# The last block of four down projections run as two column halves, with the norm chain and the next stage's entry beside the second half

## What is computed

```python
# first block, twice (i = 0: convolution, i = 1: differential attention)
f = swiglu(rms_norm(h, g0), w_gu, w_down);  h = h + 0.5 * rms_norm(f, g1)
m = mixer(rms_norm(h, g2));                 h = h + rms_norm(m, g3)
f = swiglu(rms_norm(h, g4), w_gu, w_down);  h = h + 0.5 * rms_norm(f, g5)
# second block, once
h = h + mix(rmsnorm(h, g6) @ w_in) @ w_out  # gated linear attention and dilated attention
h = h + square(relu(rmsnorm(h, g7) @ w_ff1)) @ w_ff2;  out = rmsnorm(h, g8)
```

## Time and profile before

| | |
|---|---|
| median of 3 runs (lowest, highest) | 1375.8 us (1375.73, 1375.89) |
| the profiled execution, its span | 1376.72 us, 1375.0 us |
| PE matmul busy | 1356.9 us, 99% of the span, 11028 records |
| PE weight loads busy | 1331.0 us, 97% |
| VectorE, ScalarE, GpSimd busy | 885.3 us (64%), 653.0 us (47%), 13.5 us (1%) |
| the chain that ended last | PE 94%, VectorE 3%, ScalarE 2%, DMA 1% |
| HBM | 225.49 MB read, 165 GB/s over the span |

### The profile page before, as it was taken

How to read it: one execution, slowest core, us unless ns; L and a number is a source line. 1 busy time by engine, 2 the same in 40 slices (tenths; PEclk the granted TensorE clock), 3 DMA queues, 4 the chain that set the end, 5 groups by cost and what they waited for, 6 DMA issues and landing times.

```text
span 1375.0 us, 26722 instructions
## 1 busy us (share of the span) xinstructions
PE 1356.9 (99%) x11028; PEld 1331.0 (97%) x11028; DVE 885.3 (64%) x1306; ACT 653.0 (47%) x927; POOL 13.5 (1%) x27
## 2 busy tenths in 40 slices
PE   8999999999999999999999999999999999999997
PEld 8999999999999999999999999999999999999997
DVE  6666548767666547666547897866645767777543
ACT  5444445436444445344445666644445545644332
POOL 0000000000000000000000000000001000000000
PEclk9999999999999999999999999999999999999999
DMA  7545553334445543445553323455645513455550
GB/s 285 184 166 204 202 192 139 138 123 153 171 167 216 181 147 128 162 175 210 182 190 133 123 93 124 153 184 183 234 180 195 200 62 114 163 184 183 184 184 31
DMA packets 30415, 227.68 MB, mean 166 GB/s; under 512 B 3489, under 2 KB 5089, under 8 KB 6529
## 3 DMA queue, kind: packets, MB, share of 16 engines
q1 hardware_dynamic: 28768, 223.88, 45.5%
q0 software_dynamic: 720, 1.82, 0.4%
q10 hardware_dynamic: 848, 0.87, 0.2%
HBM read 225.49 MB, written 1.06 MB: 165 GB/s over the span
## 4 chain that ended last, share of the span: by engine, by line
PE 94%; DVE 3%; ACT 2%; DMA 1%; issue 1%; ACTq 0%; DVEq 0%
PE ps L1701 26%; PE ps L1703 26%; PE ps L1702 26%; PE ps L1741 1%; PE ps L1736 1%; PE ps L1737 1%; ACT w_hi L526 1%; PE ps L1770 1%; PE ps L1761 1%; PE ps L1717 1%; PE ps L1961 1%; PE ps L1759 1%; PE ps L1937 1%; DMA w_raw<-w_gu 1%; PE ps L2200 1%
## 5 line engine op out<-in xcount | busy, mean ns | idle before, releaser
L1009 DVE TENSOR_TENSOR w_lo<-w_raw,w_hi 128x2048 fp32r<-128x2048 f32 (+2 forms) x172 | 439.0, 2553 | 207.6 <-ACT w_hi L526 207.5
L526 ACT ACTIVATE w_hi<-w_raw 128x2048 fp32r<-128x2048 f32 (+2 forms) x178 | 382.1, 2147 | 385.0 <-PE ps L1703 371.8
L1701 PE MATMUL ps<-x_hi,w_hi 128*128 128x272 f32 (+1 forms) x1952 | 561.5, 288 | 0.1
L1703 PE MATMUL ps<-x_hi,w_lo 128*128 128x272 f32 (+1 forms) x1952 | 558.6, 286 | 0.0
L1702 PE MATMUL ps<-x_lo,w_hi 128*128 128x272 f32 (+1 forms) x1952 | 556.9, 285 | 0.0
L1701 PEld LDWEIGHTS ps<-x_hi,w_hi 128*128 128x128 f32 x1952 | 367.9, 188 | 4.4 <-issue 4.0
L1703 PEld LDWEIGHTS ps<-x_hi,w_lo 128*128 128x128 f32 x1952 | 367.9, 188 | 0.0
L1702 PEld LDWEIGHTS ps<-x_lo,w_hi 128*128 128x128 f32 x1952 | 367.6, 188 | 0.1
L1701 PE MATMUL ps<-hid_hi,w_hi 128*128 128x272 f32 (+1 forms) x960 | 274.3, 286 | 0.2 <-DVE w_lo L1009 0.2
L1703 PE MATMUL ps<-hid_hi,w_lo 128*128 128x272 f32 (+1 forms) x960 | 273.6, 285 | 0.0
L1702 PE MATMUL ps<-hid_lo,w_hi 128*128 128x272 f32 (+1 forms) x960 | 272.8, 284 | 0.0
(11 more groups left out here) (308 smaller groups left out, 1416.0 us busy)
## 6 DMA issues: line engine op xcount, KB each, us to landing
w_raw<-w_gu SPq DMA_DIRECT2D x86, 1024.0 KB, 4.9
w_raw<-w_dn SPq DMA_DIRECT2D x32, 1408.0 KB, 6.0
w_raw<-w_ff SPq DMA_DIRECT2D x32, 1024.0 KB, 4.9
w_raw<-w_conv_in SPq DMA_DIRECT2D x8, 1536.0 KB, 6.6
w_raw<-w_qkv SPq DMA_DIRECT2D x8, 1536.0 KB, 6.6
w_raw<-w_mix_in SPq DMA_DIRECT2D x8, 1536.0 KB, 6.6
w_raw<-w_conv_out SPq DMA_DIRECT2D x4, 1024.0 KB, 4.9
w_raw<-w_attn_out SPq DMA_DIRECT2D x4, 1024.0 KB, 4.9
```

Of the source, the lines that this page charges most:

```text
L526: act.activation(w_hi[j % SPLIT][:, 0:width], w_raw[j][:, 0:width], ACT.Copy).then_inc(hi_ready, 1)
L1009: dve.tensor_tensor(w_lo[j % SPLIT][:, 0:width], w_raw[j][:, 0:width], w_hi[j % SPLIT][:, 0:width].bitcast(F32), ALU.subtract).then_inc(lo ...
L1701: pe.matmul(out_ap, w_hi[slot][:, cols], hi(k), start=first, stop=False)
L1703: mm = pe.matmul(out_ap, w_lo[slot][:, cols], hi(k), start=False, stop=last)
```

## The change

In the four ffn sub-blocks u = 0, 2, 3, 5 (CROSSED) the last of the 8 down blocks runs first over the lower half of the columns (136 of 272, or 128 of 256), then over the upper half, into another PSUM bank. The norm chain of the lower half is issued beside the upper half of the block; `sum_first_half` stands ahead of tile k = 5 of the second half. The next stage's entry (`first_block` for conv_in, qkv and mix_in, `first_pair` for the gu stages) goes over the 8 tiles of the lower half and then over those of the upper half, each with its own matmul; `sum_second_half` stands behind its first tile. `keep_warm` is no longer issued in these four places. ScalarE's order there is `crossing`: half-width x_hi tiles with the split of the next block's weights in three (or two) pieces between them. VectorE goes through the 8 tiles twice in half width, with the second half's Newton steps behind the first pass.

In all gu entries but the first (q = 2, 3, 5) the first two weight blocks are laid out anew on the host, as the first stage has them: block 0 holds the tiles k = 0 to 3 of all four outputs, block 1 the tiles k = 4 to 7. Their 96 matmuls stay 96 where no half is cut (q = 2 and 5); only the 16 with w_lo of block 1 stay in full width behind a cut (q = 3). VectorE's first `take` then waits for both blocks.

```diff
--- before.py
+++ after.py
@@ -340,6 +343,14 @@
 
         STATE_BANK = (6, 7, 5)
 
+        CROSSED = (0, 2, 3, 5)
+
+        GU_ENTRIES = (2, 3, 5)
+
+        LAST_BANK = {0: 4, 2: 0, 3: 4, 5: 4}
+
+        SUMS_AT = 5
+
         AHEAD = 4
 
         FIRST_SQUARES = 4
...
@@ -389,6 +400,20 @@
         def first_col(u):
 
             return 0 if u <= 4 else META
+
+        def spans(u):
+
+            c0 = META if u >= 4 else 0
+            mid = (c0 + T) // 2
+            return [(c0, mid), (mid, T)] if u in CROSSED else [(c0, T)]
+
+        def h_done(q):
+
+            return sum(KD * len(spans(u)) for u in range(q))
+
+        def x_done(q):
+
+            return KD + h_done(q - 1) if q > 0 else 0
 
         def loop(eng, count, body, first=0, peel=0):
 
...
@@ -598,6 +640,48 @@
                 act.activation(fx[:, m if isinstance(m, int) else bass.ds(m, 1), c0:T], ps[:, j, c0:T],
                                ACT.Copy, scale=g).then_inc(f_ready, 1)
 
+            def crossing(u, post, pre):
+
+                (c0, mid), _ = spans(u)
+                at, m, q, bank = CROSSED.index(u) + 1, KD - 1, u + 1, LAST_BANK[u]
+                pre_g, post_g = COL[pre], par[:, COL[post] + m:COL[post] + m + 1]
+                last_square = square[m % 2]
+
+                def x_part(i, k):
+                    a, b = spans(u)[i]
+                    act.wait_ge(h_ready, h_done(u) + KD * i + k + 1)
+                    act.activation(x_hi[:, k, a:b], h[:, k, a:b], ACT.Copy, scale=par[:, pre_g + k:pre_g + k + 1])\
+                       .then_inc(x_hi_ready, 1)
+
+                act.wait_ge(sumsq_ready, KD * u + m)
+                act.wait_ge(last_half, at)
+                act.activation(last_square[:, c0:mid], ps[:, m % 4, c0:mid], ACT.Square).then_inc(half_sq_ready, 1)
+                act.wait_ge(half_summed, at)
+                act.activation(r0[:, c0:mid], ps[:, SUM + 1, c0:mid], ACT.Abs_reciprocal_sqrt, scale=1.0 / D, bias=eps_col)\
+                   .then_inc(half_r0_ready, 1)
+                act.activation(fx[:, m, c0:mid], ps[:, m % 4, c0:mid], ACT.Copy, scale=post_g).then_inc(half_f_ready, 1)
+                x_part(0, 0)
+                x_part(0, 1)
+                act.wait_ge(block_used, FIRST[ENTER[q]])
+                act.activation(last_square[:, mid:T], ps[:, bank, mid:T], ACT.Square).then_inc(f_sq_ready, 1)
+                x_part(0, 2)
+                second_hi_part(q, 0)
+                root(None, mid, SUM, sumsq_summed, u + 1)
+                x_part(0, 3)
+                x_part(0, 4)
+                second_hi_part(q, 1)
+                act.activation(fx[:, m, mid:T], ps[:, bank, mid:T], ACT.Copy, scale=post_g).then_inc(f_ready, 1)
+                x_part(0, 5)
+                x_part(0, 6)
+                if WIDTH[FIRST[ENTER[q]] + 1] == 3 * KD * P:
+                    second_hi_part(q, 2)
+                x_part(0, 7)
+                for k in range(KD + 1):
+                    if k < KD:
+                        x_part(1, k)
+                    if k > 0:
+                        h_square(q, k - 1, c0)
+
...
@@ -1081,27 +1169,70 @@
                     qkv_lo(2, 0, 1)
                 root(s, c0, SUM)
 
...
+                if crossed:
+                    first_root()
+                else:
+                    root(s, spans(u)[0][0], SUM + 1)
+                for i, (a, b) in enumerate(spans(u)):
+                    if i == 1:
+                        dve.wait_ge(rstd_ready, s + 1)
+                    for k in range(KD + 2):
+                        if k < KD:
+                            if crossed and k == KD - 1:
+                                dve.wait_ge(half_f_ready if i == 0 else f_ready, at + 1 if i == 0 else KD * (u + 1) + F_CREDIT)
+                            if k >= 2:
+                                dve.wait_ge(h_ready, base + KD * i + k - 1)
+                            dve.tensor_tensor(scaled[k % 2][:, a:b], fx[:, k, a:b], rstd[:, a:b], ALU.mult)\
+                               .then_inc(scaled_ready, 1)
+                        if crossed and i == 0 and k >= KD - 1:
+                            second_root(k - KD + 1)
                         if k >= 2:
...
+                            lo_part(u + 1, k - 2, a, gain, b, i)
+                        if k < KD:
+                            dve.wait_ge(scaled_ready, base + KD * i + k + 1)
+                            dve.scalar_tensor_tensor(out=h[:, k, a:b], in0=scaled[k % 2][:, a:b], scalar=factor,
+                                                     in1=h[:, k, a:b], op0=ALU.mult, op1=ALU.add).then_inc(h_ready, 1)
 
...
@@ -1723,31 +1854,62 @@
                 pe.wait_ge(h_sq_copied, q + 1)
                 pe.matmul(ps[:, SUM, c0:T], ones[:, :], h_sum[:, c0:T], start=True, stop=q < 8).then_inc(h_sq_summed, 1)
 
-            def first_block(q, n0, parts, ahead=()):
-
+            def first_block(q, n0, parts):
 
                 split_ready(n0, 0)
...
+                ranges = spans(q - 1) if q < 7 else [(META, T)]
+                for i, (a, b) in enumerate(ranges):
+                    for k in range(KD):
+                        pe.wait_ge(x_hi_ready, x_done(q) + KD * i + k + 1)
+                        for s, (o, c) in enumerate(parts):
+                            cols, r = slice((s * KD + k) * P, (s * KD + k + 1) * P), slice(max(a, c), b)
+                            to = o[:, r.start - c:r.stop - c]
+                            pe.matmul(to, w_hi[0][:, cols], x_hi[:, k, r], start=i == 0 and k == 0, stop=False)
+                            pe.matmul(to, w_lo[0][:, cols], x_hi[:, k, r], start=False, stop=False)
+                        if i == 0 and k == 0 and len(ranges) > 1:
+                            sum_second_half(q - 1)
+                        pe.wait_ge(x_lo_ready, x_done(q) + KD * i + k + 1)
+                        for s, (o, c) in enumerate(parts):
+                            cols, r = slice((s * KD + k) * P, (s * KD + k + 1) * P), slice(max(a, c), b)
+                            to = o[:, r.start - c:r.stop - c]
+                            mm = pe.matmul(to, w_hi[0][:, cols], x_lo[:, k, r], start=False, stop=i == len(ranges) - 1 and k == KD - 1)
+                mm.then_inc(block_used, 1)
+
+            def first_pair(q, n0, c0):
+
+                outs = [ps[:, bank, :] for bank in (AHEAD, AHEAD + 1, 2, 3)]
+                tile_at = lambda k, s: slice((k % (KD // 2) * 4 + s) * P, (k % (KD // 2) * 4 + s + 1) * P)
+                split_ready(n0, 0)
+                ranges = spans(q - 1)
+                for i, (a, b) in enumerate(ranges):
+                    for k in range(KD):
+                        slot = k // (KD // 2)
+                        if i == 0 and k == KD // 2:
+                            pe.wait_ge(half_hi_ready, GU_ENTRIES.index(q) + 1)
+                        if i == 0 and k == KD // 2 + 2:
+                            pe.wait_ge(hi_ready, n0 + 2)
+                        pe.wait_ge(x_hi_ready, x_done(q) + KD * i + k + 1)
+                        for s, o in enumerate(outs):
+                            pe.matmul(o[:, a:b], w_hi[slot][:, tile_at(k, s)], x_hi[:, k, a:b], start=i == 0 and k == 0, stop=False)
+                            if slot == 0:
+                                pe.matmul(o[:, a:b], w_lo[0][:, tile_at(k, s)], x_hi[:, k, a:b], start=False, stop=False)
+                        if i == 0 and k == 0 and len(ranges) > 1:
+                            sum_second_half(q - 1)
+                        pe.wait_ge(x_lo_ready, x_done(q) + KD * i + k + 1)
+                        for s, o in enumerate(outs):
+                            mm = pe.matmul(o[:, a:b], w_hi[slot][:, tile_at(k, s)], x_lo[:, k, a:b], start=False, stop=False)
+                        if i == len(ranges) - 1 and k == KD // 2 - 1:
+                            mm.then_inc(block_used, 1)
+                group_squares(q, c0)
+                split_ready(n0, 1)
+                for k in range(KD // 2, KD):
+                    for s, o in enumerate(outs):
+                        mm = pe.matmul(o[:, c0:T], w_lo[1][:, tile_at(k, s)], x_hi[:, k, c0:T], start=False, stop=k == KD - 1)
+                    if k == KD // 2 + 1:
+                        sum_groups(q, c0)
+                mm.then_inc(block_used, 1)
+
+            def second_block(q, n0, outs, c0, late=False):
 
                 pe.wait_ge(hi_ready, n0 + 2)
                 if not late:
...
@@ -1828,13 +1986,40 @@
                     before = (lambda k: pe.wait_ge(hid_lo_ready, KF * f + k + 1) if k >= KF - 4 else None) if j == 0 else None
                     product(ps[:, j, c0:T], j % 2, 0, KF, hi, lo, before=before).then_inc(block_used, 1)
 
-                loop(pe, DN_N, step)
+                loop(pe, DN_N - 1 if u in CROSSED else DN_N, step)
+                if u in CROSSED:
+                    (a, mid), _ = spans(u)
+                    m = DN_N - 1
```

(26 more changed lines are left out.)

151 lines of the change are left out of this document (84 added, 67 removed).

## The result

The changed kernel takes 1412.4 us (four runs, 1412.40 to 1412.59) against 1375.85 us (four runs, 1375.73 to 1376.05): +36.6 us, a ratio of 1.0265 [1.0253, 1.0277]. Forecast were 1413.5 us and a range of 1400 to 1434.

A forecast was written before the change was run, and what follows sets the result against it. PE was taken as the bound: matmul count times spacing, plus waits. Terms 55.6 - 20.25 + 3.6 - 1.3 gave +37.7 us, so 1413.5 us against 1375.8, range 1400 to 1434.

The forecast's parts named there:

- The bound: PE, busy 99% of the span at full clock: time is matmul count times start-to-start spacing, plus PE's waits.
- Halved matmuls, +55.6: Last down blocks and entries: 560 matmuls become 1120, each half costing its 128-column weight load, 0.1115 us: +55.6 us.
- Stretches, -20.25: Four stretches between block and next entry vanish, as PE's upper half covers the lower half's norm chain: -20.25 us.
- Sums, +3.6: The norm's fp32 sum matmuls, now half width and in PE's stream, add 0.9 us at each of four places.
- small waits, -1.3: PE's small waits in the crossed entries go, since half-width VectorE delivers tiles sooner than PE needs them: -1.3 us.
- ScalarE's queue, 0 (up to 4): At the crossings, ScalarE's root waits and split pieces between x_hi tiles delay PE by 0, at most 1 us a place.
- The uncut gu entries, 0 (within 0.5): Entries q = 2 and 5, 96 matmuls before and after, VectorE's first take later: 0, within 0.5 us either way.
- Rival 1: In the halved matmuls fp32r loads hide entirely, halves cost 0.063 us, the chain then bounds: 1372 us, chance 0.07.
- The second: In the halved matmuls partly overlapping loads give a spacing about the break-even, hardly any change: some 1378 us, chance 0.03.
- Rival 3, the clock: PE's clock falls to half speed in the crossings, without empty matmuls and with PE waiting for loads: 1470 us, chance 0.06.

The follow-up runs named there:

- third: Kernel before with only the last down block of the four ffn sub-blocks run in column halves, norm chain still behind both: 1401.5 us, ratio 1.0185.
- fourth experiment: Kernel before with only the entries of conv_in, gu2, qkv and mix_in run in column halves, x tiles still full width: 1407.2 us, ratio 1.0259.
- fifth experiment: Changed kernel with CROSSED empty and the empty matmuls back, so nothing halved, new entry loops and weight layout kept: 1374.7 us, ratio 0.9990.
- first: Kernel before with 80 instead of 26 empty fp32r matmuls in each of six stretches, at 32 to 240 moving columns: 1417.3 us.
- ninth: Changed kernel with the column cut at 96 instead of the middle: 1502.4 us (1484.3 to 1513.9).

## Why the prediction was right, point by point

**The bound.** PE's stream set the time before and sets it after; the earlier trace rows against the page above.

**The segments.** From the first record of one `group_squares` to that of the next, the kernel before against the changed one. The gu entries have 8 more matmuls in front of that mark than before, 1.0 us, which is moved back in the last column but one.

| segment, to stage | before | after | difference, mark moved back | by the prediction's terms |
| --- | --- | --- | --- | --- |
| conv_in (crossed) | 205.23 | 214.24 | +9.01 | +8.97 |
| gu1 | 104.32 | 104.88 | -0.45 | 0 |
| gu2 (crossed) | 207.02 | 216.55 | +9.53 | +9.48 |
| qkv (crossed) | 206.68 | 214.77 | +9.10 | +9.05 |
| gu3 | 130.94 | 131.36 | -0.53 | 0 |
| mix_in (crossed) | 194.43 | 203.64 | +10.16 | +10.17 |

The right column is worked out for each place as in the prediction: for conv_in 138 x 0.097 - 5.11 + 0.89 - 0.20. The four crossed places are right within 0.05 us each.

**Halved matmuls, +55.6.** Right. The spacing is 0.1119 against the 0.1115 taken from the small fp32 matmuls, over 1152 records +0.5 us. The two parts by themselves measured 25.5 and 31.1 us, the second with about 1 us a place that VectorE's full width costs. The argument behind it, that the load's columns are the floor, stood the test at four load widths and six moving widths, as far as the clock held.

**Stretches, -20.25.** Right: all four are gone, and no wait has taken their place. By subtraction of the third and fourth experiments the crossing gives back 20.0 us, in which the small terms are netted: the sums and gu2's eight further halved matmuls against it, VectorE's pace and the new order of the entries for it. So that 20.0 lies so near 20.25 proves less than the windows without a wait. x_hi comes 4.6 us after the lower half's end, against 5.0 worked out.

**Sums, +3.6, and small waits, -1.3.** Not measured one by one; the segments leave their net no room for more than a tenth of a microsecond or two in any crossed place. That the waits depend on the half-width VectorE, as the term said, shows in the fourth experiment: there the segments are 0.3 to 0.7 us longer than the halves' spacing alone makes them, where the term has them 0.2 to 0.6 shorter.

**ScalarE's queue, 0 (up to 4).** Right, with a wait of 2.08 us on VectorE that didn't reach PE.

**The uncut gu entries, 0 (within 0.5).** Mis-sized: -0.45 and -0.53. The new order in these entries is worth half a microsecond each, which the fifth experiment shows without any crossing: there the same two segments give -0.46 and -0.53, gu2's -0.47, and the runs -1.3 us. In gu2 it is no addition to the sum, since the entry's small wait of 0.58 us was already counted as gone. These two make 1.0 of the 1.1 us between +37.7 and +36.6. Which instruction of the new order gives it stays open.

**The first 20 us** vary in these profiles by themselves: the first `group_squares` starts at 19.96 in the profile of before, at 18.83 in that of after and in between in others, with the same instructions ahead of it. The 0.9 us by which the profiled run of before lay above the median were most likely in this place; the runs at the median left no trace.

**Rival 1 and 2.** The first got its price (1372.2 us), though its working gives 1375, and its condition is refuted: 128 columns of four-byte weights cost 0.112 us, not below 0.079. The second needed a spacing near 0.079 and is refuted by the same rows.

**Rival 3, the clock.** It didn't happen in the changed kernel, whose four runs all have a granted clock of 0.998 or 0.999, and here there was some luck: the chance of 0.06 was low for what the runs show. The argument against it was that small fp32 matmuls keep their spacing, and it was weak: that stretch lasts 4.5 us, and in the first and ninth experiments narrow matmuls too keep 0.112 us for some microseconds before the fall. With 136 and 128 columns the clock holds for the 15.4 us of a block and the 16.4 of an entry, with 120 too; with 96 it doesn't. And one of the four runs of the fourth experiment, with halves of 136 and 128 columns, had a clock of 0.988 and took 14 us more, so even that width isn't shown to be safe. So the forecast rested on a condition that no row of before could bear out. Why the lower level comes at 96 and not at 120, and why in that one run, isn't settled by these runs.

## What to carry to other kernels

Splitting a matmul over its columns doesn't split its weight load. Before a loop is halved to hide a chain, compare: with 128x128 weights of four bytes every split costs 2 x 0.112 - 0.126 = 0.098 us here, so the 138 splits that hide a stretch of 5 us cost 13.5. With 64 weight columns, at 0.063 us a half, the splits are nearly free, and then the chain itself is the bound: 3.8 us won of 20. In bf16 a half costs 0.059 us, but no run here splits a bf16 stream. Look at the clock as well before such a stream is made narrow: with 96 columns and below it fell here, and that cost more than all the rest.

## What the runs showed of the hardware

- The granted clock fell in streams in which PE was never idle: with 128x128 fp32r weights and 96, 64 or 32 moving columns the spacing went from 0.112 to 0.213 us after some microseconds (granted clock down to 0.50, the 1.2 GHz level), and the lower level went on into matmuls of 176 columns. With 120 columns and more it stayed at 1.00 in every trace here; one run without a trace, with halves of 136 and 128 columns, had a mean clock of 0.988 and took 14 us more than its three fellows.
- After a wait of 3.7 us (26 empty matmuls left out) the lower level held for 6.0 us of full work.
- fp32r matmuls of 136 columns by load: 0.062 us (32 weight columns), 0.063 (64), 0.085 (96), 0.112 (128), the last also when the same weights are loaded again and again; bf16 with 128: 0.059. With 256 moving columns: 0.113 us beside 64 weight columns, 0.118 beside 128.
